# Second block of a two-block model: values centred as they are turned to tokens, head norms' sums and factors as quarter-array products between two gate blocks

## What is computed

```
kk = heads(k * k_k)
kk = kk / jnp.maximum(jnp.sqrt(jnp.sum(kk * kk, axis=-1, keepdims=True)), 1e-12)   # norm over a head
...
y = wkv7_scan(r_h, w_h, k_h, v_h, kk, a_h)   # S_t = S_{t-1}(...) + v_t k_t^T ;  y_t = S_t r_t
mean = jnp.mean(y, axis=-1, keepdims=True)
var = jnp.mean(jnp.square(y - mean), axis=-1, keepdims=True)
y = (y - mean) * lax.rsqrt(var + EPS_GN)
y = y.reshape(B, S, D_RWKV) * lnx_g + lnx_b
bonus = jnp.sum(r_h * k_h * r_k, axis=-1, keepdims=True) * v_h
y = (y + bonus) * g
```

## Time and profile before

| | |
|---|---|
| median of 3 runs | 2925.84 us (2925.13 to 2927.65) |
| span of the profiled execution | 2918.1 us; 7.7 us less than the median of the runs, which also hold what lies around the span |
| PE busy | 2791.1 us, 96% of the span |
| DVE / ACT / POOL busy | 1587.6 (54%) / 988.9 (34%) / 200.0 us (7%) |
| chain that ended last | PE 91%, DVE 4%, ACT 3%, issue 2% |

### The profile page before, as it was taken

One profiled execution on the slowest core, in us unless ns is written; L12 is line 12 of the kernel. 1 busy time (PEld: TensorE's weight loads), 2 busy tenths in 40 slices (PEclk: granted clock), 3 DMA queues, 4 the chain that ended last, 5 costly groups with the idle time before them and its releaser, 6 DMA issues.

```text
span 2918.1 us, 46007 instructions
## 1 busy us (share of the span) xinstructions
PE 2791.1 (96%) x19577; PEld 2317.3 (79%) x19577; DVE 1587.6 (54%) x2309; ACT 988.9 (34%) x1354; POOL 200.0 (7%) x251
## 2 busy tenths in 40 slices
PE   8899999999999999998899999999988999999998
PEld 7778888897788888777878788887667778888887
DVE  5658777854677777465443553334575443543334
ACT  5643222335532212333333332223533333332223
POOL 4100000000000000010040000000020030000000
PEclk9999999999999999799999999999889999999999
DMA  4334555421145554210022322322220013223222
GB/s 150 101 104 131 180 165 173 156 64 53 52 130 177 176 168 152 66 58 12 3 77 89 99 90 98 101 97 72 72 64 6 24 52 101 95 93 101 95 93 72
DMA packets 238532, 281.98 MB, mean 97 GB/s; under 512 B 7444, under 2 KB 224856, under 8 KB 238344
## 3 DMA queue, kind: packets, MB, share of 16 engines
q1 hardware_dynamic: 225312, 227.07, 24.3%
q0 software_dynamic: 12896, 52.11, 6.0%
q10 hardware_dynamic: 136, 0.03, 0.0%
HBM read 277.09 MB, written 2.10 MB: 96 GB/s over the span
## 4 chain that ended last, share of the span: by engine, by line
PE 91%; DVE 4%; ACT 3%; issue 2%; DMA 0%; ACTq 0%; DVEq 0%; POOL 0%; POOLq 0%
PE psum L2386 25%; PE psum L2388 25%; PE psum L2387 25%; PE psum L2445 1%; PE psum L2446 1%; PE psum L2447 1%; PE psum L2887 1%; PE psum L2902 1%; DVE wlo L1522 1%; PE psum L2484 1%; PE psum L2870 1%; PE psum L2797 1%; ACT whi L848 1%; PE psum L2821 1%; PE psum L2835 1%
## 5 line engine op out<-in xcount | busy, mean ns | idle before, releaser
L2386 PE MATMUL psum<-hh,whi 128*128 128x512 f32 (+1 forms) x2040 | 794.4, 389 | 19.5 <-DVE hl L1562 6.6
L1522 DVE TENSOR_TENSOR wlo<-raw,whi 128x2048 fp32r<-128x2048 f32 x222 | 517.3, 2330 | 514.7 <-ACT whi L848 514.1
L2387 PE MATMUL psum<-hl,whi 128*128 128x512 f32 (+1 forms) x2040 | 787.6, 386 | 0.0
L2388 PE MATMUL psum<-hh,wlo 128*128 128x512 f32 (+1 forms) x2040 | 786.9, 386 | 0.0
L848 ACT ACTIVATE whi<-raw 128x2048 fp32r<-128x2048 f32 x222 | 423.8, 1909 | 550.7 <-PE psum L2388 550.7
L2386 PE MATMUL psum<-mh,whi 128*128 128x512 f32 (+1 forms) x1248 | 486.3, 390 | 3.1 <-issue 2.3
L2387 PE MATMUL psum<-ml,whi 128*128 128x512 f32 (+1 forms) x1248 | 480.1, 385 | 0.0
L2388 PE MATMUL psum<-mh,wlo 128*128 128x512 f32 (+1 forms) x1248 | 479.8, 384 | 0.0
L2386 PEld LDWEIGHTS psum<-hh,whi 128*128 128x128 f32 x2040 | 388.1, 190 | 104.0 <-issue 25.2
L2388 PEld LDWEIGHTS psum<-hh,wlo 128*128 128x128 f32 x2040 | 387.8, 190 | 76.9
L2387 PEld LDWEIGHTS psum<-hl,whi 128*128 128x128 f32 x2040 | 388.0, 190 | 75.9 <-issue 1.0
(11 more groups left out here) (451 smaller groups left out, 2848.0 us busy)
## 6 DMA issues: line engine op xcount, KB each, us to landing
rest<-in_ada_w POOLq DMA_DIRECT2D x64, 768.0 KB, 5.3
raw<-in_w_gu SPq DMA_DIRECT2D x44, 1024.0 KB, 5.1
raw<-in_w_in SPq DMA_DIRECT2D x34, 1024.0 KB, 5.2
raw<-in_w_mlp_in SPq DMA_DIRECT2D x32, 1024.0 KB, 5.4
raw<-in_w_mlp_out SPq DMA_DIRECT2D x32, 1024.0 KB, 5.1
raw<-in_w_out SPq DMA_DIRECT2D x16, 1024.0 KB, 5.1
raw<-in_w_down SPq DMA_DIRECT2D x16, 1024.0 KB, 5.1
raw<-in_w_mem_kv SPq DMA_DIRECT2D x8, 1024.0 KB, 5.2
```

Of the source, the lines that this page charges most:

```text
L1522: ins = dve.tensor_tensor(wlo[:, g % 2, :, :], raw[:, g % 2, :, :], f32(whi[:, g % 2, :, :]), ALU.subtract)
L2386: pe.matmul(out, whi_, xhi, start=first, stop=False)
L2387: pe.matmul(out, whi_, xlo, start=False, stop=False)
L2388: return pe.matmul(out, wlo_, xhi, start=False, stop=last)
```

## The change

1. The values alone (x = 3) are turned to tokens by a product with `cent` = identity minus head mean in place of the transpose with the identity. The `gmean` products, DVE's subtraction and the matrix `mean_64` go.
2. `head_sums` is four products: tile `t` against `hsum` (128 x 32, a column of ones for each head, 30 zero columns), into partitions 32t to 32t+31 of one bank, with 512 tokens moving. The sums then lie on 2 rows of each group of 32, tokens along the row.
3. Root, bound and inverse work on a whole tile `HR` (128 x 512) in place of `hn` (128 x 32); the 1/64 of the variance is the root's scale.
4. `head_factors` is one product per tile: 32 rows of `HR` against 32 rows of `hexp`, 128 x 512, each tile into its own bank.
5. Behind the recurrence: block 0 of `g0`, `gvar`, block 1 of `g0`, `gr` 0 to 3, `g` 0 to 3. ACT takes the root ahead of the sigmoids.
6. POOL makes the three constant matrices at the start of the program; POOL, DVE and ACT have no other new place to wait.

```
-            for t in range(4):
-                self.add("gmean", l, t)
-            self.lin("g0", (l, 0), 1)
+            self.block("g0", (l, 0), 0, 0)
             self.add("gvar", l)
-            for t in range(2):
-                self.add("g", l, t)
+            self.block("g0", (l, 0), 0, 1)
             for t in range(4):
                 self.add("gr", l, t)
-            for t in range(2, 4):
+            for t in range(4):
                 self.add("g", l, t)
...
+        HR = carve(rest, o + 2 * T + 4 * HD, T)
...
+            q.step(pool.tensor_tensor(cent[:, :], ident[:, :], cent[:, :], ALU.subtract))
...
+            q.step(pool.memset(hsum[:, :], 0.0))
+            q.step(pool.memset(hsum[0:HD, 0:1], 1.0))
+            q.step(pool.memset(hsum[HD:P, 1:2], 1.0))
+            q.step(pool.memset(hexp[:, :], 0.0))
+            for a in range(0, P, 32):
+                q.step(pool.memset(hexp[a:a + 2, HD:P], 1.0))
+                q.step(pool.memset(hexp[a:a + 1, HD:P], 0.0))
+                q.step(pool.memset(hexp[a:a + 1, 0:HD], 1.0))
...
-                free(act.activation(hn[:, 0, :], bank(j)[:, 0:32], ACT.Sqrt), j)
+                free(act.activation(HR, bank(j), ACT.Sqrt), j)
...
+                j = J["gvar", l]
+                ready(act, j)
+                free(act.activation(HR, bank(j), ACT.Sqrt, scale=1.0 / HD, bias=epst[:, 1:2]), j)
                 for b in range(2):
                     j = J["g0", (l, 0), 0, b]
                     ready(act, j)
                     free(act.activation(KK[:, b, :], bank(j), ACT.Sigmoid), j)
-                j = J["gvar", l]
-                ready(act, j)
-                free(act.activation(hn[:, 0, :], bank(j)[:, 0:32], ACT.Sqrt, bias=epst[:, 1:2]), j)
...
-                q.mark(dve.tensor_scalar(hn[:, 0, :], hn[:, 0, :], 1e-12, None, ALU.max))
+                q.mark(dve.tensor_scalar(HR, HR, 1e-12, None, ALU.max))
                 q.settle()
-                dve.reciprocal(hn[:, 1, :], hn[:, 0, :]).then_inc(S("kk_inv"), 1)
+                dve.reciprocal(HR, HR).then_inc(S("kk_inv"), 1)
...
-                for t in range(4):
-                    j = J["gmean", l, t]
-                    ready(dve, j)
-                    free(dve.tensor_tensor(R2[:, t, :], R2[:, t, :], bank(j), ALU.subtract), j)
                 lo(plan.slab["g1", (l, 0), 0])
                 evacuated(dve, J["gvar", l])
-                dve.reciprocal(hn[:, 1, :], hn[:, 0, :]).then_inc(S("gn_inv"), 1)
+                dve.reciprocal(HR, HR).then_inc(S("gn_inv"), 1)
...
-                def head_sums(p, ones, src):
-
-                    for b in range(NT):
-                        for t in range(4):
-                            ins = pe.matmul(p[:, 8 * b + 2 * t:8 * b + 2 * t + 2], src[:, t, b * P:(b + 1) * P], ones[:, 0:P:HD],
-                                            start=True, stop=True)
+                def head_sums(p, src):
+
+                    for t in range(4):
+                        ins = pe.matmul(p[32 * t:32 * t + 32, :], hsum[:, :], src[:, t, :], start=True, stop=True)
                     return ins
 
                 def head_factors(p, t):
 
-                    for b in range(NT):
-                        for i in range(2):
-                            f = hn[:, 1, 8 * b + 2 * t + i:8 * b + 2 * t + i + 1].to_broadcast([P, HD])
-                            ins = pe.matmul(p[half[i], b * P:(b + 1) * P], f, ident[:, :], start=True, stop=True)
-                    return ins
+                    a = slice(32 * t, 32 * t + 32)
+                    return pe.matmul(p, hexp[a, :], HR[a, :], start=True, stop=True)
...
-                        ins = pe.transpose(p[:, t * P:(t + 1) * P], src[:, t, m * P:(m + 1) * P], ident[:, :])
+                        part, left = p[:, t * P:(t + 1) * P], src[:, t, m * P:(m + 1) * P]
+                        if x == 3:
+                            ins = pe.matmul(part, left, cent[:, :], start=True, stop=True)
+                        else:
+                            ins = pe.transpose(part, left, ident[:, :])
...
-                for i in range(2):
-                    evacuated(pe, J["Y", l, NT - 1, i])
-                for t in range(4):
-                    p = start("gmean", l, t)
-                    done(pe.matmul(p, mean_64[:, :], R2[:, t, :], start=True, stop=True))
-                linear("g0", (l, 0), 0, h)
+                linear("g0", (l, 0), 0, h, only=0)
                 pe.wait_ge(S("gn_sq"), 4 * l + 4)
-                done(head_sums(start("gvar", l), mean_64, GQ))
+                done(head_sums(start("gvar", l), GQ))
+                linear("g0", (l, 0), 0, h, only=1)
...
-                gate(0)
-                gate(1)
                 pe.wait_ge(S("gn_inv"), l + 1)
                 for t in range(4):
                     done(head_factors(start("gr", l, t), t))
-                gate(2)
-                gate(3)
+                for t in range(4):
+                    gate(t)
```

More of the change, by code:

```diff
@@ L359, in program @@
         mean_128 = sb("mean_128", [P, P])
-        mean_64 = sb("mean_64", [P, P])
+        cent = sb("cent", [P, P])
         sum_64 = sb("sum_64", [P, P])
+        hsum = sb("hsum", [P, 32])
+        hexp = sb("hexp", [P, P])
         ones = sb("ones", [P, 8])
@@ L391, in program @@
         lf = sb("lf", [P, 2, NT * FOX_H], F32R)
-        sb("padding", [P, 112])
+        sb("padding", [P, 80])
         e = ExitStack()
@@ L720, in _ @@
             q.step(pool.memset(mean_128[:, :], 1.0 / P))
-            for m, v in ((mean_64, 1.0 / HD), (sum_64, 1.0)):
+            for m, v in ((cent, 1.0 / HD), (sum_64, 1.0)):
                 q.step(pool.memset(m[:, :], 0.0))
@@ L768, in _ @@
             pool.tensor_tensor(lvl[:, :, :], lvl2[:, :, 0:CH], lvl2[:, :, CH:P], ALU.add).then_inc(s_const, 1)
+            q.step(pool.memset(hsum[:, :], 0.0))
[6 more added lines that the diff above has]
+                q.step(pool.memset(hexp[a:a + 1, 0:HD], 1.0))
+            pool.sem_inc(S("head_consts"), 1)
             pool.sem_inc(hid_done, 2)
@@ L1391, in _ @@
                 y_out(NT - 1)
+                for i in range(2):
+                    evacuated(act, J["Y", l, NT - 1, i])
                 for t in range(4):
-                    evacuated(act, J["gmean", l, t])
                     act.activation(GQ[:, t, :], R2[:, t, :], ACT.Square).then_inc(S("gn_sq"), 1)
                 hi(plan.slab["g1", (l, 0), 0])
+                j = J["gvar", l]
+                ready(act, j)
+                free(act.activation(HR, bank(j), ACT.Sqrt, scale=1.0 / HD, bias=epst[:, 1:2]), j)
                 for b in range(2):
@@ L2802, in _ @@
                 pe.wait_ge(S("kk_sq"), l + 1)
-                done(head_sums(start("kn", l), sum_64, X1))
+                pe.wait_ge(S("head_consts"), 1)
+                done(head_sums(start("kn", l), X1))
                 linear("r2", l, 1, h, only=0)
```

## The result

| | before | changed |
|---|---|---|
| median, first chip | 2925.49 us (4 runs, 2923.75 to 2927.65) | 2893.77 us (4 runs, 2890.36 to 2896.48) |
| ratio | | 0.9889, 95% interval 0.9875 to 0.9903 |
| median, another chip (repeated below) | 2921.39 us (7 runs) | 2892.47 us (4 runs), ratio 0.9894, 0.9878 to 0.9911 |
| span of the profiled execution | 2918.1 us | 2894.9 us |
| PE busy in the profiled execution | 2791.1 us | 2758.8 us |

The account below looks back on a forecast made before the run. TensorE was taken to carry the chain nearly everywhere, though DVE sets the key norm's end. Gains of 28.9 and 5.7, less 1.5 clock and 3.4 centring, made 29.7: 2925.84 to 2896 us, range 2886 to 2912.

Parts of the forecast that it names:

- The sum: Whole kernel: 28.9 behind the recurrence plus 5.7 at the key norm, less 1.5 clock and 3.4 centring, 29.7 us gained.
- the stretch behind the recurrence: From Y's read-out to slab g1: 22.6 us, gaining 15.3 and 13.6 in the two layers, 28.9 together.
- Strips at once: Sums and factors: four quarters of the array work together, 1.1 us for each group of four products, bounds 0.92 and 3.67.
- Clock: From the sums to slab g1 behind the recurrence: clock 1.00, where 0.50 followed the two-column sums before.
- The rival in which the clock falls ahead of the gates: Behind the recurrence: gates and factors double, 9.5 us a layer; one layer 2906, both 2915; chance 0.20.
- The wait for the inverse: TensorE, ahead of the factors behind the recurrence: inverse ends at 13.0, 1.0 us behind block 1 of g0.
- the sign of being wrong that the prediction named: Behind the recurrence: TensorE waiting for POOL's windows, expected to end at 31.3 us and be wanted at 33.5, 2.2 left.
- Key norm: Ahead of the recurrence: DVE's row sets the gain, 3.6 and 2.1 us in the two layers, 5.7 together; bounds 0 and 17.4.
- Idle time ahead of the recurrence: TensorE's gap grows from 2.2 to about 5 us, costing 0.75 more low clock per layer, 1.5 together.
- Centring: Four centring products take 1.0 us against 0.59 for transposes: 0.42 more, eight times, 3.4 in all, mostly on the path.
- The conversion to a median: Profiled span to median of runs: span 7.7 us below the median, so 2925.84 less 29.7 gives 2896.
- The rival of strips in turn: Sums and factors: strips work one after another, 3.67 us each, total gain 18.7, giving 2907; chance 0.12.

Follow-up runs that it names:

- One quarter alone: Changed kernel with the factor products of all four tiles reading rows 0 to 31 of the inverted roots, sums keeping four strips: 2906.70 us, ratio 0.9948.
- the pair of kernels with the same stretch filled in two ways: Changed kernel plus, ahead of the factors behind the recurrence, 16 two-column sums (2910.38 us, ratio 0.9952) or five dense 128x512 products (2895.87 us, ratio 0.9900).
- the repeated run: The changed kernel timed again, unaltered, beside the kernel before on another chip: 2892.47 us, ratio 0.9894.
- old order: Changed kernel's new products in the earlier order (both blocks of g0, sums, gates 0 and 1, factors, gates 2 and 3): 2893.99 us, ratio 0.9907.
- both inverses first: Changed kernel with root and inverse ahead of slab g1's parts, DVE's key scaling ahead of a low part, one preparation behind A2: 2883.10 us, ratio 0.9872.
- gates' half: Changed kernel with, behind the recurrence only, the root ahead of slab g1's high part and the inverse ahead of its low part: 2892.64 us, ratio 0.9904.
- the old key norm: Changed kernel with the key norm's two-column sums, 128 x 32 root and inverse, and broadcast-column factors put back: 2899.39 us, ratio 0.9928.
- the new order of DVE: Changed kernel with DVE scaling keys ahead of a v2 low part, one preparation behind A2: 2879.65 us alone, 2883.10 with the gates' order changed too.
- the key norm's half: Changed kernel with only DVE's key scaling moved ahead of the first v2 slab's low part and one preparation behind A2: 2879.65 us, ratio 0.9857.

## Why the prediction was right, and where it was off

- **The sum.** Right by its mechanism, with two errors that offset each other in part: the stretch behind the recurrence gave 2.1 less than forecast, the key norm 0.7 more. The stretches give 28.2 for 29.7; the medians give 31.7 and 28.9, and that they stand so close on both sides is in part luck, as the kernel before alone moved over 11 us in 19 runs on one chip.
- **Strips at once.** Right: 1.06 and 1.14 for 1.1 and 1.1. One quarter alone gives 3.67, the same as products over the whole array. Four row strips bring a factor of 3.2, four column strips 3.5. The Trainium skill's TensorE: Matmul & The Clock Gate (Part 3) has 3.07 for the former; the measurement stands close above it, well below the 3.9 that I read from L2870 in the earlier trace rows.
- **Clock.** Right: 1.00 from the sums to g1, in both layers and in both profiles of the changed kernel. The cause that I named, the narrow sums, holds by the pair of kernels with the same stretch filled in two ways. The rival in which the clock falls ahead of the gates had a price of 9.5 a layer; made to happen, it cost 10.4 and 11.0 (with 2.2 for the added products).
- **The wait for the inverse** was mis-sized: 1.81 in place of 1.0. The sum put the low part at 2.38 and its end at 9.7; it took 3.08 and ended at 10.5, as the slab's chain started 0.1 later and a POOL step (L810) had started 0.1 ahead of the low part, which again ended 2.15 behind that step. With 0.25 of issue the stage is 23.6 and not 22.6, so 26.8 were gained of 28.9. The size depends on which of the two starts first: in the first layer of the kernel without centring and in the repeated run the low part was 0.17 and 0.03 ahead and took 2.29, POOL's step took 3.02 and 3.16 in place of 1.04, and TensorE waited 0.74 and 0.90. It costs the kernel nothing that the runs can show, though: where it is gone, TensorE waits for POOL's windows, the nearness of which was named (2.2 left). POOL ended them 35.6 behind the read-out, not 31.3: two of its copies took 2.13 and others 0.53, where 0.19 is what they take alone. In the three kernels that remove the wait ahead of the factors (old order, both inverses first, gates' half) the sign of being wrong that the prediction named, TensorE waiting for POOL's windows, does come: 0.5 to 1.2.
- **Key norm.** 4.0 and 2.4 measured for 3.6 and 2.1, in the two parts that were forecast: the end of the low part moved by 1.6 and 1.2 (1.45 and 1.0), and behind it 1.7 are left in place of 4.1 and 3.0 (1.9), since TensorE has made the inputs by then. That DVE's row decides there and not TensorE's whole saving is shown twice: by the old key norm (34.0 again) and by the new order of DVE, which moved the first strict product by 3.3 in each layer and the end with it. The low part stayed long beside POOL's key scaling, as said, 6.02 here and 5.38 in the new order; each ended 2.15 behind POOL.
- **Idle time ahead of the recurrence** grew from 2.2 to 5.3, in two pieces: 1.17 for POOL's key scaling ahead of L2866 and 4.14 for DVE ahead of L2894; about 5 was forecast. 0.75 a layer was put for more low clock: over the first 5 us behind the idle time the clock was 0.66 before and is 0.54 now, 0.6 more lost in the first layer:

```profile
1292.00:1297.00 5.00, 5.00 (x74) 4.13 (x75) 4.25 (x7) 0.66 (x2) 0.00 (x0) 0.66 0.01 3
```

```profile
1292.60:1297.60 5.00, 5.00 (x72) 4.26 (x73) 3.80 (x7) 0.66 (x2) 0.00 (x0) 0.54 0.29 98
```

  The recurrences took 4.9 more, as forecast (1.5 + 3.4). How this splits is settled only roughly: without centring they took 347.0 together, before 346.3, with it 351.3, and in the kernel before with centring alone 352.1.
- **Centring.** 1.09 for 1.0 in each step, so 0.5 more than the transposes, 4.0 in all for 3.4.
- **The conversion to a median** went wrong and did no harm. I took the 7.7 us between the profiled span of 2918.1 and the median as lying around the span. Every run has only 1.6 there; that execution must have been some 6 us faster than the median. A difference of stretches added to the median is sound for all that.
- The rival of strips in turn gave 2907, and the kernel that makes them go in turn in the factors gave 2906.7, but for another reason: 14.2 more than the changed kernel's 2892.47 (on another chip), of which 2.5 behind each recurrence is the factors' own time and the rest is clock.

## What to carry to other kernels

Look at the clock behind small products, not only at their own time: 4.3 us of two-column products cost 8.6 us more in the factors and gates that followed. Group them so that all four quarters work at once. Before hiding a wait, ask what stands 1 to 2 us behind it: two ways to take away the 1.8 us wait gave nothing, while the row of an engine that never looked full (DVE, 55% busy) gave 11 to 13. And read two engines that work side by side in pairs: the length of DVE's low part was set by POOL's step beside it, and POOL's step by DVE's before it.

## What the runs showed of the hardware

- Float32 products over 32 rows, one after another, brought the clock to 0.50 within the eight records or right behind them in three places of four (3.67 us at full speed, 5.06 where it fell inside), while the same eight records over four strips (1.14 us) left it at 1.00. In the same kernels gates that alternate 128 and 32 rows leave it at either level.
- A POOL copy of 128x2 took 0.18, 0.53 or 2.13 us, the last beside a low part of DVE (3.08 in the changed kernel, 2.38 in the kernel before), and ended within 0.1 of it. The Trainium skill's SBUF — State Buffer (SBUF: two separate sides) has the two engines exclude each other, and lets the second wait for the whole instruction of the first. The traces agree: POOL's key scaling ended 4.44 to 4.48 behind the end of DVE's step that had started 0.12 ahead of it, and DVE's low part 2.15 behind POOL. It is a cost that sums of durations miss.
- The spread of a kernel follows how often the clock falls: 3 us between the slowest and fastest run of the key norm's half (mean clock 0.979 to 0.981), 17 and 29 where the narrow sums or the single quarter bring it down (0.969 to 0.976, and 0.970 to 0.980).
